# Transposes behind V products: the order of TensorE's work within a step of four attention mixers

## The chip, the cores and the metric

One core of one Trainium2 chip runs the whole program. The metric is device time in microseconds (us), lower is better; a time of a kernel is the median of several executions. A core has a matrix engine (TensorE, PE in the profile, its weight loads PEld), a vector engine (VectorE, DVE), a scalar engine (ScalarE, ACT), GpSimd (POOL) and SyncE (SP), each with its own instruction queue worked in program order, synchronized by semaphores.

## What is computed

Two transformer blocks over 512 tokens of width 1024. The change lies in the second block, in its softmax mixers: differential attention, attention with a forget gate ("fox"), and sparse attention ("nsa") with three branches (compressed, selected, window). All have this form, cut from the reference:

```python
# differential attention: two softmax maps per head
s = jnp.einsum('bhqmd,bhkmd->bhmqk', qb, k) * scale + bias;  p = softmax(where(dist >= 0, s, NEG))
w = p[:, :, 0] - lam * p[:, :, 1]
o = jnp.einsum('bhqk,bhkd->bhqd', w, v)
# forgetting attention: bias is cq - cum; one map per head
# sparse attention: o = g0 * softmax(cmp) @ vc + g1 * softmax(sel) @ v_slc + g2 * softmax(win) @ v_win
```

## The kernel before

The mixers' work is a list `MIX` of 40 items. An item is one block of 128 queries (`t` of 0 to 3), for one pair of heads (e = 0, 1), against w = (t+1)*128 keys. The order of the blocks is t = 3, 0, 2, 1, so the widths are 512, 128, 384, 256. Items 0 to 7 are differential ("diff", four score maps each: two per head), 8 to 15 fox (two maps), 16 to 39 nsa: for each of two pairs of heads and each t, a compressed branch of 31 keys ("cmp"), then the selected and the window branch of width w (two maps each).

Each engine runs a loop over steps n and works on items of different age:

- TensorE, `mixers_pe` (L1929): `scores(MIX[n])` writes each map to one of four PSUM banks (L1938); `turn(MIX[n-2])` transposes the probabilities in 128x128 pieces into banks 4 (e = 0) and 5 (e = 1) (L1950); `times_v(MIX[n-3])` multiplies V by the turned probabilities into bank 6 or 7 (L1961). At n = 0 it also spreads the forget gate (L1972).
- VectorE, `mixers_dve` (L1979): `front(n)` adds the bias to the scores and takes the row's minimum of the negated sum (L1992), writing into `SRING`, a ring of 8 maps; `back(n-1)` makes reciprocals and probabilities (L1999 to L2022).
- ScalarE, `mixers_act` (L2031): `exps(n)` (L2039), then `keep(n-2)`, the copies of the turned probabilities from banks 4 and 5 to `PTR`, which has two buffers (L2048), then `keep_out(n-4)`, the output of a pair of heads (L2054).
- GpSimd, `fox_bias_pool` (L2069): the biases of the fox items, two buffers (L2080, L2082); its third item waits until `front` of the first fox item has read its own.

The waits that tie them: `scores` waits until `front` has read the bank four maps before. `turn(n-2)` waits, for each half e, for the probabilities of item n-2 (`mx_probs`) and for `mx_kept` of item n-3's half e, since it writes the bank which that copy empties. `times_v(n-3)` waits for both copies of item n-3 (`mx_kept`, 2n+2 by its own n). `front` waits, from map 8 on, for the transposes (`mx_turned`) of the item that used its place in the ring eight maps before: for diff items, item n-2. `keep` waits for its transposes and for the V products two items before.

After the mixers follow a fourth mixer (stick-breaking, `stick_pe`) and the rest of the block.

Of the kernel before, what the change touches and what calls it, by code (L numbers as in the profile page):

```python
# [159 lines left out]
def build_program(nc, A, out):  # L160

    ctx = ExitStack()
    with ctx:
# [1464 lines left out]
        def cst2(name):  # L1628
            o, w = c2_at[name]
            return C2[:, o:o + w]  # L1630
# [292 lines left out]
        MIX = mixer_items()  # L1923
# [5 lines left out]
        def mixers_pe(pe):  # L1929

            sel4 = cst2("sel4").rearrange("p (h m) -> p h m", h=4)

            def scores(it):
                for k, (l, r, _) in enumerate(it["maps"]):
                    j = it["j0"] + k
                    if j >= 4:
                        pe.wait_ge(mx_shifted, j - 3)
                    nc.tensor.matmul(ps[:, j % 4, 0:it["w"]], l, r, start=True, stop=True).then_inc(mx_scores, 1)  # L1938

            def turn(it):  # L1940
                n = it["n"]
                for e in range(2):
                    pe.wait_ge(mx_probs, 2 * n + e + 1)
                    if n == 0:
                        pe.wait_ge(fox_kept, 4)
                    else:
                        pe.wait_ge(mx_kept, 2 * n + e - 1)
                    src = SRING[:, (it["j0"] + e) % 8, :]
                    for i, (c0, m) in enumerate(it["blocks"]):
                        last = nc.tensor.transpose(ps[0:m, 4 + e, i * P:(i + 1) * P], src[:, c0:c0 + m], ident)  # L1950
                    last.then_inc(mx_turned, 1)

            def times_v(it):
                n, t = it["n"], it["t"]
                pe.wait_ge(mx_kept, 2 * n + 2)
                if it["begins"] and it["pair"] >= 2:
                    pe.wait_ge(mx_out_kept, it["pair"] - 1)
                nb = len(it["blocks"])
                for x, (c0, m) in enumerate(it["blocks"]):
                    for e in range(2):  # L1960
                        last = nc.tensor.matmul(ps[64 * e:64 * e + 64, 6 + it["pair"] % 2, t * P:(t + 1) * P],  # L1961
                                                it["v_of"](e, x), PTR[0:m, n % 2, e, x, :],
                                                start=it["begins"] and x == 0, stop=it["ends"] and x == nb - 1)
                last.then_inc(mx_pv, 1)

            for n in range(len(MIX) + 3):
                if n < len(MIX):
                    scores(MIX[n])
                if n == 0:

                    for h in range(4):
                        nc.tensor.matmul(ps[:, 4 + h, :], sel4[0:4, h, :], FL[0:4, 1, :], start=True,  # L1972
                                         stop=True).then_inc(fox_spread, 1)
                if 2 <= n < len(MIX) + 2:
                    turn(MIX[n - 2])
                if n >= 3:
                    times_v(MIX[n - 3])

        def mixers_dve(v):  # L1979

# [495 lines left out]
        def _(eng):  # L2476
# [46 lines left out]
            qk_norm_pe(pe)  # L2523
            pe.stage_end()
            mixers_pe(pe)
            pe.stage_end()
            stick_pe(pe)
# [41 lines left out]
```

## Time and profile before

| | us |
|---|---|
| median of 3 runs | 1983.44 |
| lowest, highest of them | 1979.52, 1989.31 |
| the profiled execution's own time | 1981.9 |
| its span, first to last instruction | 1979.8 |
| the mixers' steps in it (L1938 to L1961) | 118.5 |
| TensorE busy in the span | 1746.8 |
| VectorE busy | 946.2 |
| ScalarE busy | 624.8 |

The profile is of one execution. A row of the timeline has start, duration, engine, line, operation, output and inputs, shapes, count, and in brackets the idle time of the engine before it with what ended it. TensorE's ends are modelled, so its busy time is not work at its peak; starts are what to read. Where several instructions were merged, the row gives the first start and the count.

### The profile page before, as it was taken

To read this page: it belongs to the slowest core of one execution; us is meant where nothing else is said; L and a number is where in the kernel's file an instruction comes from. 1 tells how busy PE (TensorE), PEld (TensorE's weight loads), DVE (VectorE), ACT (ScalarE), POOL (GpSimd) and SP (SyncE) were. 2 spreads that over 40 slices of the span, in tenths; PEclk is the share of its full clock that TensorE was granted. 3 is DMA by queue.
4 is the path that set the end of the run, shared out by engine and by line. 5 is a ranking of instruction groups with operands and counts; after the bars stand their busy time and mean duration, and the time that the engine had idled before them with its cause. 6 is when DMAs were issued, how large, how long until landed. Compare 5 with 4: busy or idle time off the path is not lost.

```text
span 1979.8 us, 26555 instructions
## 1 busy us (share of the span) xinstructions
PE 1746.8 (88%) x11544; PEld 1400.2 (71%) x11544; DVE 946.2 (48%) x1447; ACT 624.8 (32%) x900; POOL 34.4 (2%) x50
## 2 busy tenths in 40 slices
PE   3999765986889889999999689998876879999998
PEld 2888434983779578888888478875544768888886
DVE  4135658623334434555454632245754455554644
ACT  2221143224233415424231122244764222222220
POOL 0000000000000000000000000001300000000000
PEclk9999887997999999999999899976987889999999
DMA  4322200001224133455454422320000223323322
GB/s 136 102 89 88 85 12 1 4 4 34 73 64 154 39 127 109 143 176 183 135 201 160 134 64 75 97 44 1 1 1 0 66 63 86 107 86 106 88 93 74
DMA packets 149029, 163.62 MB, mean 83 GB/s; under 512 B 14704, under 2 KB 110306, under 8 KB 148786
## 3 DMA queue, kind: packets, MB, share of 16 engines
q1 hardware_dynamic: 141896, 152.10, 24.2%
q10 hardware_dynamic: 7018, 9.83, 1.7%
q8 instruction: 91, 1.49, 0.3%
q14 instruction: 24, 0.20, 0.0%
HBM read 159.79 MB, written 2.13 MB: 82 GB/s over the span
## 4 chain that ended last, share of the span: by engine, by line
PE 74%; DVE 6%; ACT 4%; issue 2%; POOL 1%; DMA 1%; DVEq 1%; ACTq 0%; POOLq 0%
PE ps L370 54%; PE ps L1031 4%; PE ps L1157 2%; PE ps L630 2%; PE ps L2121 1%; PE ps L1950 1%; PE ps L1938 1%; PE ps L1961 1%; PE ps L1335 1%; PE ps L1811 1%; POOL sb_hT L2080 1%; DVEq L156 1%; PE ps L1767 1%; ACT sb_hT L2039 1%; PE ps L1809 1%
## 5 line engine op out<-in xcount | busy, mean ns | idle before, releaser
L390 DVE TENSOR_TENSOR weights_low<-sb_weights_raw,weights_high 128x2048 fp32r<-128x2048 f32 (+3 forms) x119 | 266.6, 2241 | 376.5 <-ACT weights_high L387 376.2
L370 PE MATMUL ps<-left_high,weights_high 128*128 128x512 f32 x1032 | 405.4, 393 | 19.0 <-DVEq L156 7.5
L370 PE MATMUL ps<-left_low,weights_high 128*128 128x512 f32 x1032 | 403.9, 391 | 0.0
L370 PE MATMUL ps<-left_high,weights_low 128*128 128x512 f32 x1032 | 403.6, 391 | 0.0
L387 ACT CAST weights_high<-sb_weights_raw 128x2048 fp32r<-128x2048 f32 (+3 forms) x119 | 222.2, 1868 | 446.4 <-PE ps L370 437.6
L370 PEld LDWEIGHTS ps<-left_high,weights_high 128*128 128x128 f32 x1032 | 193.7, 188 | 61.9 <-DVEq L156 8.1
L370 PEld LDWEIGHTS ps<-left_high,weights_low 128*128 128x128 f32 x1032 | 193.7, 188 | 42.7
L370 PEld LDWEIGHTS ps<-left_low,weights_high 128*128 128x128 f32 x1032 | 193.9, 188 | 41.6
L370 PE MATMUL ps<-weights_high,hidden_high 128*128 128x512 f32 x432 | 168.9, 391 | 0.0
L370 PE MATMUL ps<-weights_high,hidden_low 128*128 128x512 f32 x432 | 168.2, 389 | 0.0
L370 PE MATMUL ps<-weights_low,hidden_high 128*128 128x512 f32 x432 | 168.1, 389 | 0.0
L370 PE MATMUL ps<-weights_high,left_high 128*128 128x512 f32 (+2 forms) x352 | 125.6, 357 | 26.1 <-DVE left_low L649 26.1
L370 PE MATMUL ps<-weights_low,left_high 128*128 128x512 f32 (+2 forms) x352 | 125.1, 355 | 0.0
L370 PE MATMUL ps<-weights_high,left_low 128*128 128x512 f32 (+2 forms) x352 | 124.9, 355 | 0.0
L370 PEld LDWEIGHTS ps<-weights_high,left_high 128*128 128x128 f32 x352 | 67.9, 193 | 37.3 <-issue 28.0
L370 PEld LDWEIGHTS ps<-weights_high,hidden_low 128*128 128x128 f32 x432 | 81.1, 188 | 17.1
L370 PEld LDWEIGHTS ps<-weights_high,hidden_high 128*128 128x128 f32 x432 | 81.1, 188 | 16.7
L370 PEld LDWEIGHTS ps<-weights_low,hidden_high 128*128 128x128 f32 x432 | 81.1, 188 | 16.5
L1534 DVE TENSOR_TENSOR hidden_low<-sb_arena,hidden_high 128x512 fp32r<-128x512 f32 x54 | 37.4, 692 | 92.4 <-ACT hidden_high L1529 92.4
L370 PEld LDWEIGHTS ps<-weights_low,left_high 128*128 128x128 f32 x352 | 67.9, 193 | 9.2
L370 PEld LDWEIGHTS ps<-weights_high,left_low 128*128 128x128 f32 x352 | 67.8, 193 | 9.3
L630 PE MATMUL ps<-sb_arena,sb_X 128*128 128x128 f32 x320 | 47.1, 321 | 30.0 <-DVE sb_arena L599 30.0
(342 smaller groups left out, 2167.3 us busy)
## 6 DMA issues: line engine op xcount, KB each, us to landing
sb_weights_raw<-in_w_in SPq DMA_DIRECT2D x24, 1024.0 KB, 5.3
sb_yT<-in_ada_w SPq DMA_DIRECT2D x24, 1024.0 KB, 5.2
sb_weights_raw<-in_ffn_w_up SPq DMA_DIRECT2D x44, 512.0 KB, 4.8
sb_weights_raw<-in_mlp_w_up SPq DMA_DIRECT2D x16, 1024.0 KB, 6.0
sb_weights_raw<-in_mlp_w_down SPq DMA_DIRECT2D x16, 1024.0 KB, 7.4
sb_weights_raw<-in_ffn_w_down SPq DMA_DIRECT2D x10, 1024.0 KB, 5.0
sb_weights_raw<-in_w_out SPq DMA_DIRECT2D x8, 1024.0 KB, 5.0
sb_weights_raw<-in_xattn_w_kv SPq DMA_DIRECT2D x8, 1024.0 KB, 5.3
```

The source lines that it names most:

```text
L156: self.eng.drain().then_inc(self.stage_sem, 1)
L370: last = nc.tensor.matmul(o, lhsT, rhs, start=b["first"] and i == 0, stop=b["last"] and i == len(pairs) - 1)
L387: nc.scalar.copy(h[:, 0:n], raw[:, 0:n]).then_inc(w_high, 1)
L390: nc.vector.tensor_tensor(l[:, 0:n], raw[:, 0:n], h[:, 0:n].bitcast(F32), ALU.subtract).then_inc(w_low, 1)
L630: last = nc.tensor.matmul(ps[:, k, t * P:(t + 1) * P], src[:, t, k * P:(k + 1) * P], RDIAG[:, t, :], start=True, stop=True)
L1031: last = nc.tensor.matmul(ps[b, bank, c * 64:(c + 1) * 64], lhsT(b, u, c), rhs(b, u, c), start=True, stop=True)
L1157: last = nc.tensor.matmul(o_of(b), *own_pairs[i], start=i == 0, stop=i == len(own_pairs) - 1)
L1335: last = nc.tensor.matmul(ps[b, 6 + o % 2, q0:S], v_of(x), PT[0:m, buf, x, q0:S], start=grp["begins"] and x == 0, stop=grp["ends"] and x = ...
L1534: nc.vector.tensor_tensor(HIDL[part % 2][:, i, :], x, HIDH[part % 2][:, i, :].bitcast(F32), ALU.subtract).then_inc(ff_low, 1)
L1767: last = nc.tensor.matmul(ps[:, 4 * (i % 2) + f, :], mat, SQS[i][:, f, :], start=True, stop=True)
L1809: nc.tensor.matmul(ps[b, 1, 0:1], PHI[b, l, :], PET[b, l:l + 1], start=l == 0, stop=l == 31)
L1811: last = nc.tensor.matmul(ps[b, 2, 0:NCMP], PHI[b, l, :], KV[b, l:l + 16 * (NCMP - 1) + 1:16], start=l == 0, stop=l == 31)
```

## The change

In each step TensorE's V products of item n-3 now stand ahead of the transposes of item n-2; they stood behind them. Nothing else is changed: the waits inside `turn` and `times_v` are the same, and so are the loops of the other engines.

```diff
@@ mixers_pe, for n in range(len(MIX) + 3): after scores(MIX[n]) and, at n == 0, the forget gate's spread
+                if n >= 3:
+                    times_v(MIX[n - 3])
                 if 2 <= n < len(MIX) + 2:
                     turn(MIX[n - 2])
-                if n >= 3:
-                    times_v(MIX[n - 3])
```

## Rows read from the trace of the kernel before

**Rows 1.** The page's first line: the span.
```profile
span 1979.8 us, 26555 instructions
```

**Rows 2.** View by windows, the mixers' steps: window, its length, busy us of each engine.
```profile
1345.57:1464.11 118.54, 101.36 (x728) 60.74 (x728) 81.21 (x336) 80.49 (x282) 26.05 (x32) 0.86 0.00 1
```

**Rows 3.** Waits in that window: who waited for whom, us, times, longest.
```profile
DVE sb_hT L1992 <- PE ps L1938: 22.3, 22, 4.6
...
PE ps L1950 <- ACT sb_hT L2048: 9.1, 15, 1.3
```

**Rows 4.** View by windows, two stretches; the granted clock is third from last.
```profile
1360.00:1365.00 5.00, 3.75 (x12) 2.29 (x10) 3.21 (x13) 3.45 (x10) 2.16 (x5) 0.50 0.00 0
...
1380.00:1385.00 5.00, 3.67 (x28) 2.22 (x26) 3.57 (x16) 3.45 (x10) 0.00 (x0) 1.00 0.00 0
```

**Rows 5.** Timeline, step 3: keep(0), T(1), V(0), front(3).
```profile
1363.55 1.04 ACT L2048 COPY sb_hT<-ps 128x512 f32<-128x512 f32 x2
...
1364.25 0.93 PE L1950 MATMUL ps<-sb_consts,sb_hT 128*128 128x128 f32 x2 [0.45 <-ACT sb_hT L2048]
...
1365.11 1.98 PE L1961 MATMUL ps<-sb_hT,sb_arena 128*64 128x128 f32 x16
1365.33 0.42 DVE L1992 CUSTOM_DVE_ANT_0 sb_hT<-ps,sb_arena 128x256 f32<-128x256 f32 x1 [1.54 <-PE ps L1950]
```

**Rows 6.** Timeline, step 4: T(2); step 5: keep(2), T(3), V(2)'s loads.
```profile
1369.04 0.64 PEld L1950 LDWEIGHTS ps<-sb_consts,sb_hT 128*128 128x128 f32 x6 [1.50 <-DVE sb_hT L2013]
...
1373.64 0.83 ACT L2048 COPY sb_hT<-ps 128x384 f32<-128x384 f32 x2
...
1374.23 1.08 PE L1950 MATMUL ps<-sb_consts,sb_hT 128*128 128x128 f32 x4 [0.79 <-ACT sb_hT L2048]
1375.25 1.15 PEld L1961 LDWEIGHTS ps<-sb_hT,sb_arena 128*64 128x64 f32 x12 [0.33 <-issue]
```

**Rows 7.** Timeline, step 6: keep(3), T(4).
```profile
1377.36 0.61 ACT L2048 COPY sb_hT<-ps 128x256 f32<-128x256 f32 x2
...
1378.32 1.51 PE L1950 MATMUL ps<-sb_consts,sb_hT 128*128 128x128 f32 x8
```

**Rows 8.** Timeline, step 7: keep(4), T(5)'s second half.
```profile
1383.00 1.04 ACT L2048 COPY sb_hT<-ps 128x512 f32<-128x512 f32 x2
...
1384.18 0.30 PE L1950 MATMUL ps<-sb_consts,sb_hT 128*128 128x128 f32 x1 [0.18 <-ACT sb_hT L2048]
```

**Rows 9.** Timeline, GpSimd: first and last of 24 in the fox items.
```profile
1390.30 1.40 POOL L2080 TENSOR_SCALAR sb_hT<-sb_yT,sb_small 128x384 f32<-128x384 f32 x1 [27.96 <-DVE sb_stat L1992]
...
1410.08 0.45 POOL L2082 TENSOR_TENSOR sb_hT<-sb_hT,sb_arena 128x128 f32<-128x128 f32 x1
```

**Rows 10.** Timeline, T(17); then steps 31 to 35: T(29), S, V(29), keep(28) to keep(30).
```profile
1419.37 1.06 PE L1950 MATMUL ps<-sb_consts,sb_hT 128*128 128x128 f32 x8 [0.87 <-DVE sb_hT L2020]
...
1443.32 0.40 ACT L2048 COPY sb_hT<-ps 31x128 f32<-31x128 f32 x2
...
1443.71 1.06 PE L1950 MATMUL ps<-sb_consts,sb_hT 128*128 128x128 f32 x8 [0.65 <-DVE sb_hT L2020]
...
1444.43 1.07 ACT L2048 COPY sb_hT<-ps 128x512 f32<-128x512 f32 x2
...
1446.51 0.85 PEld L1961 LDWEIGHTS ps<-sb_hT,sb_arena 128*64 128x64 f32 x16 [0.17 <-issue]
...
1446.71 1.05 ACT L2048 COPY sb_hT<-ps 128x512 f32<-128x512 f32 x2
1447.53 0.30 PEld L1938 LDWEIGHTS ps<-sb_arena 64*128 64x128 f32 x4 [0.17 <-issue]
...
1450.39 0.30 PEld L1938 LDWEIGHTS ps<-sb_arena 64*128 64x128 f32 x4 [0.17 <-issue]
```

**Rows 11.** Timeline, the drain: T(39), V(39)'s loads.
```profile
1462.20 0.69 PE L1950 MATMUL ps<-sb_consts,sb_hT 128*128 128x128 f32 x4
...
1463.40 0.42 PEld L1961 LDWEIGHTS ps<-sb_hT,sb_arena 128*64 128x64 f32 x8 [0.17 <-ACT sb_hT L2048]
```

## Prediction

> **What bounds the kernel now.** The page gives the span, 1979.8 us [rows 1]. The view by windows puts the changed loops in 118.5 us of it, 1345.57 to 1464.11 [rows 2]; nothing outside runs code that moves. So the question is what 118.5 us become. Below, S(n) are the score products of item n, T(n) its transposes, V(n) its V products; front(n) and back(n) are VectorE's halves, exps(n) and keep(n) ScalarE's. TensorE's step n was S(n), T(n-2), V(n-3) and becomes S(n), V(n-3), T(n-2).
>
> In that window TensorE's modelled busy time is 101 us, VectorE's 81, ScalarE's 80 [rows 2]: no engine is full, they hand work round. The list of waits says how. VectorE waits 22.3 us for scores, and 15 times, 9.1 us in all, the transposes' first matmul waits for keep (L2048) [rows 3]. This second row is the one to read: T(n-2) needs keep(n-3) because it writes the two PSUM banks that keep(n-3) empties (bank 4+e only after half e), and V(n-3) needs both halves of keep(n-3). Where T already starts the moment half 0 is kept, V cannot slip in ahead without pushing it.
>
> **The change, part by part.** Instructions are the same, 40 S, 40 T and 40 V groups, with the same durations, no DMA. No wait is added in name; but V's wait for both halves of keep(n-3) now stands ahead of T(n-2). Behind it on TensorE's queue are T(n-2) and S(n+1). SP's and POOL's queues are not passed. Three waits hang on T: keep(n-2); in the diff items (4 maps of a ring of 8) front(n), which needs T(n-2); and the last V of all.
>
> New closed loop: T(n) then keep(n), both halves, then V(n), then T(n+1). Old loop: T(n) half e, keep(n) half e, T(n+1) half e. So V and a half copy are added wherever this loop is what sets the time.
>
> *Diff items, steps 3 to 8.* The loop here is front, exps, keep, T, front.
> Step 3: keep(0) ends at 1363.55+1.04=1364.59, T(1) starts at 1364.25 behind its first half, V(0) follows, front(3) starts at 1365.33 [rows 5]. After: V(0) can start about 0.16 after keep ends (T(5)'s second half starts 0.14 after keep(4) does [rows 8]), at 1364.75, and its 16 matmuls hold TensorE some 1.85 of the 1.98 us shown at the low clock; T(1)'s second half, which started at about 1364.75 before, comes with 0.17 between the groups at about 1366.8. Front(3) moves by **+2.0**.
> Step 5: keep(2) ends at 1374.47, T(3) started at 1374.23, V(2)'s loads took 1.15 us [rows 6], and front(5) waits for T(3). After: V(2) from 1374.63 for 1.15 to 1.28, T(3)'s second half at about 1376.1 instead of 1374.7. **+1.3**.
> Step 6: T(4) starts at 1378.32, keep(3) ended at 1377.97 [rows 7]. V(3), 8 matmuls of about 0.053 us each at the full clock (16 take 0.85 [rows 10]), goes from 1378.13 to 1378.55; with 0.17 us between two groups [rows 10] T(4) comes at 1378.72. **+0.5**.
> Step 7: keep(4) ends at 1384.04, T(5)'s second half at 1384.18 [rows 8]; 16 V matmuls hold 0.85 [rows 10]. After: V(4) takes T(5)'s place, T(5) at 1385.2. **+1.1**.
> Steps 4 and 8: T(2) started at 1369.04 on VectorE's last probabilities, after 1.50 us without a load [rows 6], and T(6) likewise; keep plus the short V (0.20 us) ends before that, so V fits; I take +0.1 for both. Sum of the diff items **+5.0**. Bounds: if the clock is full in steps 3 and 5, V(0) costs half and the sum is 3.6; if low in all, V(3) and V(4) cost twice and the sum is 6.4.
>
> *Fox items.* POOL builds the bias tiles from 1390.30 to 1410.53 with no gap over 0.1 us [rows 9], and front waits for them at the end. POOL's start hangs on front(8), so the +5.0 passes on whole, but nothing is added: 0 (upper bound 0.8, if front(10) is late for the fifth pair of tiles). This is the cover; were it gone, T's in steps 9 to 15 would be late as in the next part.
>
> *Nsa items: two periods of 12 steps, 24.3 us each.* I walk the second, items 28 to 39; the first has the same rows 24.34 us earlier (T(17) at 1419.37, T(29) at 1443.71 [rows 10]). Step 31: keep(28) ends at 1443.72, T(29) starts at 1443.71 [rows 10]; V(28), four small matmuls, now goes ahead from 1443.88, and T(29) starts at 1444.35, +0.64. Keep(29), before at 1444.43 for 1.07 us, starts when T's first half is done, 1445.0, and ends 1446.1. Step 32: V(29) must wait for that, 1446.25, and hold 0.85; before, T(30) ran during keep(29). T(30) comes at 1447.27, S(33) at 1448.3 against 1447.53: +0.8. Step 33: keep(30) starts at 1447.87 against 1446.71, takes 1.05, V(30) ends at 1449.95, T(31) follows, S(34) at 1450.48: +1.2. Step 34: T(31), its keep of 0.4, V(31) and T(32) in a row; S(35) at 1451.75 against 1450.39: +1.4. From there VectorE's chain leads, and steps 37 and 38 add 0.2 in the same way. A period adds **+1.6**, two, less 0.1 counted twice at the seam, **+3.1**. Bounds: 0.8 a period if only step 32's exposed wait stays (later ones soaked by VectorE), 2.2 if the late S(35) also pushes the 384-wide pieces: 1.6 to 4.4 in all.
>
> *The drain.* T(39) at 1462.20, then keep(39), then V(39)'s second load block at 1463.40 [rows 11], 1.2 us after T. After: V(37) stands ahead of T(38) (+0.55) and V(38), which waits for keep(38), ahead of T(39), which comes at about 1463.7; V(39) at 1464.9. **+1.5** (bounds 0.6, V(37) and V(38) alone, and 1.8).
>
> **Sum.** 5.0 + 0 + 3.1 + 1.5 = 9.6 us, lost. The profiled execution took 1981.9 us, span 1979.8; 1981.9 + 9.6 = 1991.5. The three runs' median, 1983.44, is 1.5 above that execution, so about 1992 to 1993; I say **1992**. A 0.5% difference, 9.9 us, is about what a measurement of this kernel can tell from none (its own three runs lie 9.8 us apart).
>
> **The clock.** Granted clock is 0.50 (1.2 GHz) from 1360 to 1365, and 1.00 (2.4 GHz) from 1380 to 1385 [rows 4]; the climb lies within the stage, and every group of matmuls there costs twice at the low level (16 V matmuls: 1.98 against 0.85 [rows 5, 10]). The change adds idle TensorE time in just these steps; the sum keeps each step's clock as it was. The Trainium skill (TensorE: Matmul & The Clock Gate, "What's actually happening") says that the throttled state is the default and activity releases it. The rows agree: the low level follows the sparse steps before. By that rule extra idle time would postpone the climb, and the loss would be the 12 to 18 us of the third rival below in place of 9.6.
>
> **Rivals.**
> *V fills the idle time (not slower).* TensorE stood waiting for probabilities before most T. If V fits there, S(n+1) starts earlier by V's time and VectorE's waits for scores, 22.3 us in 22 times [rows 3], shrink. Some 16 of them are in the nsa items; by V's load time, 0.85 us for 512 keys [rows 10] and so 0.2 for 128, some 0.4 in the mean over all items, that is -6.4: 1975.5. It decides where keep(n-3) ends a full V before back(n-2). For: steps 4 and 8, and the wait by VectorE on scores. Against: the 15 T's that waited for keep itself [rows 3], and step 32, where T used the time of keep. Chance 0.05.
> *Absorbed.* VectorE's chain or POOL takes up the nsa part and half of the diff part: 0 to +5, about 1984.5. For: POOL's full 20 us; ScalarE's and VectorE's loads near 70%. Against: front(n) hangs on T(n-2) in the diff items with no slack. Chance 0.17.
> *The clock climbs later.* If the window up to about 1385 stays at 0.50, the bounds above give 6.4 for the diff items, the 26 transposes of T(2) to T(6) take up to 0.053 more each, 1.4, and S(4) to S(8) up to about 0.5 a step, an estimate: another 4, and 6.4 + 4 + 3.1 + 1.5 = 15: +12 to +18, about 1997. Chance 0.18.
> *My case*, +5 to +12: 0.60, with its own range 1987 to 1994.
>
> **How the numbers follow.** Over 9.9 us slower: 0.43 of my case (0.26), nearly all of the clock's (0.16): 0.42. Faster by over 0.5% needs more than the first rival gives: 0.02. The rest, 0.56, is within 0.5%. Range: 1983 (leaves out the first rival and a third of the second) to 2000 (leaves out the clock's upper end).
>
> **What would show it.** In the profile after: V(0) (L1961) ahead of T(1) (L1950), front(3) (L1992, 128x256) about 2 us later after keep(0); T waiting less for ScalarE, V now waiting for it (L1961 <- ACT L2048), which before it hardly did; POOL's 20.2 us unchanged; nsa period near 25.9 us instead of 24.3; the rest of the kernel as long as before. Wrong if the nsa period is no longer, if the window 1345 to 1380 has another clock, or if front in the diff items starts at the same distance from keep.

## The result and the profile after

The changed kernel takes 1995.84 us (median of 7 executions; one of them, of 2650 us at a mean clock of 0.64 and not 0.93, is left out of the comparison, and so is one of 3824 us of the filled new order below), the kernel before 1981.61 in the same comparison. The ratio is 1.0068, 95% interval 1.0047 to 1.0089: 14 us or 0.7% slower. That is inside the stated range, and beyond the 9.6 us of the likeliest case.

The profiled execution has a span of 1991.5 us. The view by windows for the mixers' steps, from the first score product to the start of the last output copy (columns as in [rows 2]; the granted clock is third from last):

```profile
1343.54:1477.28 133.74, 110.68 (x728) 67.43 (x728) 81.15 (x336) 81.80 (x281) 26.02 (x32) 0.77 0.00 1
```

133.74 us stand against 118.54 [rows 2]: +15.20, at a mean clock of 0.77 against 0.86. VectorE, ScalarE and GpSimd have the same busy time within 1.3 us. Outside the stage the two executions differ by -3.5 us (it begins 2.03 earlier, the rest behind it is 1.47 shorter), in code that is the same.

The list of waits in that window answers [rows 3]:

```profile
PEld ps L1961 <- ACT sb_hT L2048: 35.7, 39, 2.7
DVE sb_hT L1992 <- PE ps L1938: 28.3, 22, 4.6
PE ps L1961 <- ACT sb_hT L2048: 17.5, 24, 2.4
DVE sb_hT L1992 <- PE ps L1950: 16.2, 6, 3.6
...
ACT sb_hT L2048 <- PE ps L1950: 8.2, 14, 1.2
```

TensorE's wait for ScalarE's copies has moved from the transposes to the V products. The two rows with L1961 are two views of the same waits, those of the weight loads (PEld) and those of the matmuls behind them (PE), and can't be added: there are only 40 groups of V products. The loads of 39 groups wait, 35.7 us in all; the matmuls wait 17.5 us in 24 times, against 9.1 us in 15 times for the transposes before [rows 3]. (The "53 us in 63 times" of an expectation below is the sum of both rows.) Two more rows show who pays for it: VectorE's front waits 16.2 us for transposes (7.6 before), in 6 times, and ScalarE's copies 8.2 (0.9 before).

**The diff items.** Timeline, step 3, to be read against [rows 5]:

```profile
1361.52 1.04 ACT L2048 COPY sb_hT<-ps 128x512 f32<-128x512 f32 x2
...
1362.61 1.58 PEld L1961 LDWEIGHTS ps<-sb_hT,sb_arena 128*64 128x64 f32 x16 [1.55 <-ACT sb_hT L2048]
...
1364.52 0.69 PE L1950 MATMUL ps<-sb_consts,sb_hT 128*128 128x128 f32 x2
...
1365.36 0.42 DVE L1992 CUSTOM_DVE_ANT_0 sb_hT<-ps,sb_arena 128x256 f32<-128x256 f32 x1 [3.60 <-PE ps L1950]
```

V(0) starts when the second copy ends (1362.56), holds TensorE for 1.91 us to T(1)'s start, and front(3) comes 3.84 us after keep(0) began; before it was 1.78: +2.06. Here is the view by windows from each front to the next, steps 3 to 8, after:

```profile
1358.51:1365.36 6.85, 5.25 (x26) 3.80 (x26) 3.22 (x14) 3.45 (x10) 1.62 (x4) 0.50 0.01 2
1365.36:1371.38 6.02, 5.40 (x18) 3.12 (x18) 3.57 (x13) 2.43 (x10) 0.00 (x0) 0.50 0.00 1
1371.38:1378.58 7.20, 5.22 (x24) 3.85 (x24) 4.15 (x14) 3.66 (x10) 0.00 (x0) 0.50 0.00 0
1378.58:1384.30 5.72, 5.22 (x24) 3.42 (x24) 3.35 (x13) 2.17 (x10) 0.00 (x0) 0.51 0.00 0
1384.30:1391.15 6.85, 4.72 (x26) 3.04 (x26) 3.22 (x13) 3.45 (x10) 0.00 (x0) 0.74 0.00 0
1391.15:1396.36 5.21, 4.72 (x16) 2.49 (x18) 3.49 (x14) 2.86 (x11) 0.00 (x0) 0.50 0.00 0
```

and the same of before (these windows were not among the rows above):

```profile
1360.54:1365.33 4.79, 3.69 (x12) 2.51 (x14) 3.22 (x14) 3.45 (x10) 1.62 (x4) 0.50 0.00 0
1365.33:1370.07 4.74, 4.74 (x34) 2.72 (x32) 3.57 (x14) 2.43 (x10) 0.00 (x0) 0.61 0.02 5
1370.07:1375.47 5.40, 3.70 (x18) 2.23 (x16) 4.15 (x14) 3.67 (x10) 0.00 (x0) 0.72 0.00 0
1375.47:1379.99 4.52, 4.52 (x32) 2.94 (x32) 3.35 (x14) 2.17 (x10) 0.00 (x0) 0.58 0.00 0
1379.99:1384.63 4.64, 3.31 (x22) 1.86 (x20) 3.21 (x13) 3.45 (x10) 0.00 (x0) 1.00 0.00 0
1384.63:1388.89 4.26, 3.17 (x30) 1.77 (x26) 3.49 (x14) 2.87 (x11) 0.00 (x0) 1.00 0.00 0
```

The steps lose 2.06, 1.28, 1.80, 1.20, 2.21 and 0.95 us, 9.50 in all. VectorE's and ScalarE's busy times are equal row by row, within 0.01 us. The clock column is not: before, it reaches 1.00 in step 7; after, it stays at 0.50 or 0.51 to step 6 and is back at 0.50 in step 8.

The prediction took the 1.50 us without a load ahead of T(2) [rows 6] for a gap into which V(1) fits. The timeline of TensorE's matmuls before, in steps 4 and 8, shows that only one of the two steps has it:

```profile
1367.02 2.10 PE L1938 MATMUL ps<-sb_arena 32*128 32x512 f32 x8
1369.04 0.88 PE L1950 MATMUL ps<-sb_consts,sb_hT 128*128 128x128 f32 x6
...
1387.68 1.08 PE L1950 MATMUL ps<-sb_consts,sb_hT 128*128 128x128 f32 x6 [1.09 <-DVE sb_hT L2013]
```

In step 4 the loads had stopped, but S(4)'s matmuls ran until T(2) began: no idle time. After the change V(1) starts at 1369.07, as S(4) ends, and T(2) 0.62 us behind it. Ahead of T(6), in step 8, the matmuls stood idle for 1.09 us.

**The fox items.** GpSimd's first and last rows, against [rows 9]:

```profile
1397.77 1.40 POOL L2080 TENSOR_SCALAR sb_hT<-sb_yT,sb_small 128x384 f32<-128x384 f32 x1 [37.47 <-DVE sb_stat L1992]
...
1417.68 0.45 POOL L2082 TENSOR_TENSOR sb_hT<-sb_hT,sb_arena 128x128 f32<-128x128 f32 x1
```

20.36 us, before 20.23. GpSimd starts 54.2 us after the first score product (44.7 before) and adds 0.13: a full cover.

**The nsa items and the drain.** Steps 31 to 35, against [rows 10], and the drain, against [rows 11]:

```profile
1453.26 1.09 PE L1950 MATMUL ps<-sb_consts,sb_hT 128*128 128x128 f32 x8
...
1454.01 1.07 ACT L2048 COPY sb_hT<-ps 128x512 f32<-128x512 f32 x2 [0.43 <-PE ps L1950]
...
1454.29 0.30 PEld L1938 LDWEIGHTS ps<-sb_arena 64*128 64x128 f32 x4 [0.17 <-issue]
...
1455.14 0.85 PEld L1961 LDWEIGHTS ps<-sb_hT,sb_arena 128*64 128x64 f32 x16 [0.55 <-ACT sb_hT L2048]
...
1456.16 0.85 PEld L1950 LDWEIGHTS ps<-sb_consts,sb_hT 128*128 128x128 f32 x8 [0.17 <-DVE sb_hT L2020]
...
1457.18 0.30 PEld L1938 LDWEIGHTS ps<-sb_arena 64*128 64x128 f32 x4 [0.17 <-issue]
...
1460.64 0.30 PEld L1938 LDWEIGHTS ps<-sb_arena 64*128 64x128 f32 x4 [0.17 <-issue]
...
1465.90 1.02 PEld L1950 LDWEIGHTS ps<-sb_consts,sb_hT 128*128 128x128 f32 x6 [0.17 <-issue]
...
1475.35 0.42 PEld L1950 LDWEIGHTS ps<-sb_consts,sb_hT 128*128 128x128 f32 x4 [0.17 <-issue]
...
1475.88 0.65 ACT L2048 COPY sb_hT<-ps 128x256 f32<-128x256 f32 x2 [1.17 <-PE ps L1950]
...
1476.58 0.42 PEld L1961 LDWEIGHTS ps<-sb_hT,sb_arena 128*64 128x64 f32 x8 [0.81 <-ACT sb_hT L2048]
```

Behind S(32) V(29) waits 0.55 us for the end of keep(29), time in which T(30) ran before. From T(29) to S(35) it takes 7.38 us, before 6.68. From T(17) at 1427.50 to T(29) at 1453.26 one period takes 25.76 us, before 24.34: +1.42. Near the end T(35)'s six loads, at 1465.90, take 1.02 us and not the 0.64 of the full clock: it dips there. What the dip costs can be read from the same kernel, since T(23) to T(24), one period earlier, are the same instructions. View by windows, T(23) to T(24), then T(35) to T(36):

```profile
1440.14:1442.50 2.36, 2.32 (x25) 1.57 (x23) 1.45 (x8) 1.49 (x5) 0.00 (x0) 1.00 0.00 0
1465.90:1469.71 3.81, 3.81 (x24) 2.66 (x22) 1.79 (x9) 1.96 (x7) 0.00 (x0) 0.55 0.02 4
```

That is 1.45 us at a clock of 0.55. T(39) to V(39) is 1.23 us, before 1.20; what is added stands ahead of T(39). From GpSimd's last end to the stage's end it is 59.15 us against 53.58: +5.57. With 9.50 and 0.13 that makes the 15.20. Of the 5.57 us, 1.45 are the dip's, and 4.12 are left for the order.

### The profile page after: what moved, and what is told of

Its sections match the earlier page's. It is cut to its first block, busy times and chain, and to the rows that moved or that the text cites. A ratio compares the mean times of both kernels' runs of the same rounds, so it can differ in the third digit from the quotient of the medians.

```text
span 1991.5 us, 26555 instructions
## 1 busy us (share of the span) xinstructions
PE 1751.8 (88%) x11544; PEld 1404.7 (71%) x11544; DVE 946.1 (48%) x1447; ACT 626.0 (31%) x900; POOL 34.3 (2%) x50
## 4 chain that ended last, share of the span: by engine, by line
PE 74%; DVE 6%; ACT 4%; issue 2%; DMA 1%; POOL 1%; DVEq 1%; ACTq 0%; POOLq 0%
PE ps L370 54%; PE ps L1031 4%; PE ps L1157 2%; PE ps L630 2%; PE ps L1961 1%; PE ps L2121 1%; PE ps L1938 1%; PE ps L1950 1%; ACT sb_hT L2039 1%; PE ps L1335 1%; PE ps L1811 1%; DVEq L156 1%; PE ps L1767 1%; ACT sb_hT L2048 1%; PE ps L1809 1%
```

## The experiments

Two theories. *L*: the closed loop of copy, V products, transposes puts V's own time on the path wherever the loop leads. *C*: what costs is TensorE's clock. And, within L, whether it is the wait for the second copy or the time of V behind it.

**Where the loss lies.** The new order in some steps only:

```diff
+                if n >= 3 and (n <= 8):      # second kernel: (n >= 16)
+                    times_v(MIX[n - 3])
                 if 2 <= n < len(MIX) + 2:
                     turn(MIX[n - 2])
-                if n >= 3:
+                if n >= 3 and not (n <= 8):
                     times_v(MIX[n - 3])
```

> V products stand ahead of transposes in steps 3 to 8 only. If each part of the loss comes from its own steps (theory L, the closed loop of copy, V products, transposes), GpSimd starts on the fox biases some 9 us later after the first score product than before (44.7 us before, 54.2 after the change), the nsa period stays at 24.3 us, and the kernel is about 9.5 us slower than before. If the loss of the diff items is mostly a clock that would climb late by chance (theory C), it is between 3.6 and 5 us when the clock climbs as in the kernel before.

> V products stand ahead of transposes from step 16 on only. Theory L: GpSimd's start stays at 44.7 us after the first score product, the nsa period is 25.8 us instead of 24.3, the drain 1 to 1.5 us longer, 4 to 5.5 us slower in all. Theory C (only the clock's late climb costs): no measurable loss, since the clock is at its full level there.

> The changed kernel once more, for the granted clock. If its clock (0.50 until 1380 us, 0.50 again from 1390 to 1401) is a consequence of the order, it is the same within a few us here; if it is chance, the climb lies elsewhere and the diff items take 3 us or more less.

Steps 3 to 8 alone: ratio 1.0060 (1.0045 to 1.0075), some 12 us; GpSimd starts 54.2 us after the first score product, as in the changed kernel. Step 16 on alone: 1.0042 (1.0027 to 1.0057), some 8 us, GpSimd at 44.6. The whole change again: 1.0077 (1.0060 to 1.0094). The placing that theory L gives is right. But the parts add to more than the whole (1.010), and the nsa part was expected at 4 to 5.5 us. The view by windows from GpSimd's last end to the stage's end, before, then steps 3 to 8 alone, then step 16 on alone, shows why:

```profile
1410.53:1464.11 53.58, 47.92 (x434) 30.22 (x434) 38.31 (x184) 41.36 (x157) 0.01 (x1) 1.00 0.01 2
1419.33:1476.00 56.67, 50.86 (x434) 31.96 (x434) 38.28 (x184) 41.51 (x156) 0.00 (x1) 0.94 0.01 2
1410.90:1472.66 61.76, 52.76 (x434) 33.19 (x434) 38.25 (x184) 42.82 (x156) 0.00 (x0) 0.92 0.01 2
```

The changed kernel took 59.15 us there, at 0.97. With only steps 3 to 8 changed, the nsa items have the order of before and yet lose 3.09 us, at a clock of 0.94; with step 16 on changed they lose 8.18 where the whole change lost 5.57. In both a lower clock goes with the surplus, which neither theory had placed there.

The second profile of the changed kernel repeats its steps 3 to 8 to 0.01 us, the clock of each to 0.01, and so does that of steps 3 to 8 alone. The late climb is thus most likely a consequence of this instruction order: C in its form "by chance" falls; as a consequence of the order it remains.

**The wait without V's time, and V's time without the wait.** First the kernel before with one wait more:

```diff
                 n = it["n"]
+                if n:
+                    pe.wait_ge(mx_kept, 2 * n)
                 for e in range(2):
                     pe.wait_ge(mx_probs, 2 * n + e + 1)
```

> The kernel before with one more wait: the transposes of item n-2 wait for both copies of item n-3, not for the half that they overwrite. V products stay behind. This is the new order's wait without V's time ahead. If the wait is the cost, GpSimd's start moves by most of the 9.5 us; if V's time behind that wait is, by 0 to 2 us (a half copy of 0.2 to 0.5 us at steps 3, 5 and 7), and the nsa period by under 0.5 us.

Steps 3 to 8 took 28.53 us in sum, against 28.35 before and 37.85 after: the wait costs the diff items 0.2 us. In the second nsa period and the drain, all at the full clock, S(28) to the end of V(39) takes 28.2 us against 27.6. Over the kernel the ratio is 1.0023 (1.0013 to 1.0032), some 4.5 us, more than the 0 to 2 us and the half microsecond a period lead to. The first nsa period shows where most of that comes from. The view by windows, from S(19) to S(22), items 19 to 21, in this kernel, and the same of before:

```profile
1415.80:1425.84 10.04, 9.14 (x69) 7.00 (x67) 4.81 (x26) 6.50 (x24) 0.00 (x0) 0.66 0.00 0
```

```profile
1418.09:1424.98 6.89, 6.02 (x69) 4.65 (x67) 4.85 (x27) 6.23 (x24) 0.00 (x0) 1.00 0.00 0
```

The same 69 matmuls; their mean clock fell to 0.66 and the three items took 3.15 us longer. The wait as such is small where the clock is as before; a fall of the clock is not.

Then V one item older, whose copies were made a step before:

```diff
-            for n in range(len(MIX) + 3):
+            for n in range(len(MIX) + 4):
...
+                if n >= 4:
+                    times_v(MIX[n - 4])
                 if 2 <= n < len(MIX) + 2:
                     turn(MIX[n - 2])
-                if n >= 3:
-                    times_v(MIX[n - 3])
```

> V products of item n-4 instead of n-3 stand ahead of the transposes of item n-2, so that their wait for both copies is over long before. Theory L: the loss is gone, TensorE's wait of V for the copies (53 us in 63 times after the change) falls to nearly nothing, and V fills idle time: from 0 to 6 us faster than the kernel before. The rival, that V ahead of T costs by its place alone (TensorE's time ahead of the transposes), has it still 3 us or more slower than before.

Ratio 1.0011 (0.9999 to 1.0022): within noise of before, and 11 us faster than the changed kernel. The wait of V's loads for copies is down from 35.7 us to 9.5. But it isn't the gain of 0 to 6 us that was expected: in the diff items step 4, where V(0) now stands ahead of T(2), takes 7.32 us instead of 4.74 at a clock of 0.50 (0.61 before), steps 3 to 8 take 33.81 instead of 28.35, and GpSimd starts at 50.2 us. V(0) follows S(4) there without a pause and holds TensorE for 1.91 us: V's time costs with no wait before it, so the rival named in the expectation holds in these steps. In the nsa items it gains 1.9 us from GpSimd's last end on (51.72 against 53.58): from S(28) to the end of V(39) 26.4 against 27.6, while S(16) to S(28) takes 25.1 against 24.7, with a clock of 0.67 in one stretch of 5 us.

**V's time twice.** The changed kernel with the V products of items 0 to 5 issued two times over:

```diff
+                for _ in range(2 if n < 6 else 1):
-                for x, (c0, m) in enumerate(it["blocks"]):
+                    for x, (c0, m) in enumerate(it["blocks"]):
...
```

> The changed kernel with the V products of items 0 to 5 (steps 3 to 8) issued twice. If V's time stands on the path in each of these steps, the six steps grow by V's slots once more: 1.9, 0.6, 1.3, 0.9, 1.7 and 0.3 us at the low clock, near 6.5 in sum, or 3.5 if the denser work raises the clock. If the loss was the wait ahead of V and not its time, they grow by under 1.5 us in all.

The ratio to before is 1.0091 (1.0061 to 1.0120), in two executions. Steps 3 to 8 took 8.55, 5.51, 8.34, 6.20, 8.00 and 4.50 us, 41.10 in sum, 3.25 more than after, near the 3.5 expected if the clock rises. Step 3, at the same clock but for 0.01, grew by 1.70, about the time of one V(0) at 1.2 GHz. Steps 4 and 8 became shorter, at clocks of 0.79 and 1.00 in place of 0.50: with more work in TensorE's idle time the clock was back sooner. So V's time is on the path, and the clock hides part of it in the sum.

**The order at a high clock.** Matmuls whose output nobody reads were added to both orders, ahead of the mixers and in steps 1 to 6 or 7 (between S(n) and what follows it); first few, then more:

```diff
             last.then_inc(cmp_sum, 1)
+            for _ in range(4):
+                nc.tensor.matmul(ps[:, 6, :], ident, KV, start=True, stop=True)
             pe.wait_ge(cmp_sq, pe.count(cmp_sq))
...
+            FILL = {1: 2, 2: 1, 3: 1, 4: 1, 5: 1, 6: 1}   # more: {1: 3, 2: 1, 3: 2, 4: 2, 5: 3, 6: 2, 7: 2}
...
+                if n == 1:
+                    pe.wait_ge(fox_kept, 4)
+                for _ in range(FILL.get(n, 0)):
+                    nc.tensor.matmul(ps[:, 7, :], ident, QK[:, 0, :], start=True, stop=True)
```

> The kernel before with added matmuls whose output nobody reads (four of 512 columns ahead of the mixers, then two, one, one, one, one, one in the idle time of steps 1 to 6), to raise TensorE's clock in the diff items. This is the base of the pair for the order at a high clock. If fillers raise the clock, 1345 to 1385 us is at 1.00 and the stage is 0 to 4 us shorter; if not, it is up to 4 us longer.

> The changed kernel with the same fillers. If the order's own cost in the diff items is the 3.6 us that the prediction gave for the full clock and the other 6 are the clock's, GpSimd's start on the fox biases is 3 to 4.5 us later than in the filled old order; if the 9.5 us are the order's cost at any clock, it is 8 or more later.

> Old order with denser fillers (three, one, two, two, three, two, two in steps 1 to 7), to hold the clock at 1.00 through the diff items, where the first fillers let it fall in steps 5, 6 and 8. Base of a pair; front(5) to front(8) spaced as in the kernel before at the full clock (4.52, 4.64, 4.26 us), or up to 1 us more a step where a filler is in the way.

> New order with the same fillers. At clock 1.00 the first pair gave +1.08 us for step 3 and +0.52 for step 4 against +2.06 and +1.28 at 0.50. If the rest is the same, front(3) to front(8) loses 4 to 5 us in sum to the more filled old order where both clocks are at 1.00; if the order alone costs the 9.5 us, 8 or more.

As a means to a faster kernel the fillers fail: ratios 1.0056 (1.0041 to 1.0071) and 1.0061 (1.0038 to 1.0084) in the old order, 1.0137 (1.0119 to 1.0154) and 1.0135 (1.0115 to 1.0155) in the new. Nor did they hold the clock everywhere. But they give steps in which both orders run at 1.00. The windows of steps 3, 4 and 6 to 8, more filled, old order:

```profile
1366.12:1371.15 5.03, 4.41 (x18) 2.35 (x20) 3.21 (x13) 3.45 (x10) 0.00 (x0) 1.00 0.00 0
1371.15:1376.71 5.56, 5.56 (x38) 3.33 (x34) 3.57 (x14) 2.43 (x10) 0.00 (x0) 1.00 0.02 4
...
1384.83:1389.66 4.83, 4.83 (x36) 2.94 (x34) 3.34 (x13) 2.17 (x10) 0.00 (x0) 1.00 0.00 0
1389.66:1394.69 5.03, 4.85 (x26) 2.54 (x24) 3.21 (x13) 3.45 (x10) 0.00 (x0) 1.00 0.00 0
1394.69:1398.95 4.26, 3.17 (x30) 1.77 (x26) 3.49 (x14) 2.87 (x11) 0.00 (x0) 1.00 0.01 4
```

and new order:

```profile
1368.61:1374.82 6.21, 5.43 (x30) 2.90 (x30) 3.21 (x14) 3.45 (x10) 0.00 (x0) 1.00 0.01 3
1374.82:1380.89 6.07, 5.44 (x22) 2.68 (x22) 3.56 (x14) 2.43 (x10) 0.00 (x0) 1.00 0.01 1
...
1391.22:1396.79 5.57, 5.07 (x28) 2.88 (x28) 3.35 (x13) 2.17 (x10) 0.00 (x0) 1.00 0.00 0
1396.79:1404.64 7.85, 7.08 (x30) 3.33 (x30) 3.22 (x14) 3.45 (x10) 0.00 (x0) 0.78 0.01 2
1404.64:1408.92 4.28, 2.85 (x16) 1.63 (x18) 3.48 (x14) 2.86 (x11) 0.00 (x0) 1.00 0.00 0
```

At the full clock on both sides the order costs 1.18 us in step 3, 0.51 in step 4, 0.74 in step 6 and 0.02 in step 8; the first, less filled pair gave 1.08 and 0.52 for steps 3 and 4. Unfilled these four lost 2.06, 1.28, 1.20 and 0.95. So some 2.4 of 5.5 us are the order's own and the rest the clock's. This carries over to the unfilled kernels only as an estimate, since the fillers take time of their own and hide part of the waits. In steps 5 and 7 the two sides had different clocks, and their split wasn't measured. For the whole of steps 3 to 8 the expectations were missed: the new order is 7.9 us behind the old with the first fillers (37.77 against 29.84; expected were 3 to 4.5, or 8 and more) and 7.5 with more (40.31 against 32.83; expected 4 to 5, or 8 and more). In neither pair did both sides hold 1.00 throughout, so the sums decide nothing.

**A version that beats both.** The old order up to step 15, V one item older ahead of the transposes from step 16 on, where the clock is high:

```diff
+                if n > 16:
+                    times_v(MIX[n - 4])
                 if 2 <= n < len(MIX) + 2:
                     turn(MIX[n - 2])
-                if n >= 3:
+                if 3 <= n < 16:
                     times_v(MIX[n - 3])
```

> Old order up to step 15, and from step 16 on the V products of item n-4 ahead of the transposes of n-2. The nsa period with V one item older was 1.2 us shorter than before in the look at V one item older throughout, and the diff items were what lost. So 2 to 3 us faster than before if that holds, 0.15% at most; no change if the clock in the nsa items falls.

> The same with the fillers of the pair above in the diff items. Gains add: the filled old order's change to before plus 2 to 3 us less.

Ratio to before 0.9982 (0.9972 to 0.9991), 4.2 us faster by the medians (1976.78 against 1980.97), a little more than the 2 to 3 us expected; the interval lies below 1. From S(16) to S(28) it takes 22.6 us against 24.7. From GpSimd's last end to the stage's end it is 50.24 us against 53.58, both at a clock of 1.00. With fillers the ratio is 1.0032 (1.0021 to 1.0044), 4.2 us less than the filled old order: the gain adds as expected, but the fillers lose more than it gives back.

## Why the prediction was right in sign and short in size

- *No wait in name, but the wait for both copies ahead of the transposes; old and new loop.* Right. 39 of the 40 V groups wait for copies, and the two kernels with half of the change each place the loss as the steps do. The wait alone costs 0.2 us in the diff items; V's time behind it is what counts.
- *Step 3, +2.0.* 2.06. It is the one diff step whose clock was 0.50 on both sides.
- *Steps 4 and 8, +0.1 together.* 1.28 and 0.95. "V fits" holds for step 8 at the full clock (0.02) and not for step 4 (0.51 to 0.52), whose 1.50 us without a load were a pause of the loads and not of TensorE; the rest is the clock. The same two views are mixed in "costs twice at the low level (1.98 against 0.85)": 16 V matmuls take 1.98 and 1.09 us, their loads 1.58 and 0.85.
- *Steps 5, 6, 7: +1.3, +0.5, +1.1.* 1.80, 1.20, 2.21. At the full clock step 6 costs 0.74.
- *The diff items, +5.0, bounds 3.6 to 6.4.* 9.50. **This is the term that failed**, and the step of it is "the sum keeps each step's clock as it was". The prediction had seen that the change adds idle time of TensorE on the clock's way up, and gave that its own rival, with 6.4 + 4 us for these items; measured are 9.5. One of its own signs of being wrong came: from 1345 to 1380 us the clock is 0.50, where it was 0.56. The bounds of the term itself doubled V's cost alone and not that of the transposes behind it: T(2)'s loads take 1.14 us where they took 0.64.
- *The fox items, 0.* 0.13 us. GpSimd's chain passes the delay on and adds nothing.
- *A nsa period, +1.6.* +1.42 from T(17) to T(29), V(29)'s exposed wait in its place. From T(29) to S(35) the walk is right to 0.02 us (7.40, measured 7.38); the 0.2 too much lies behind it.
- *The drain, +1.5.* With both periods and the seam, 5.57 us against 4.6. The clock's dip around 1466 us accounts for 1.45 of them, by the same instructions a period earlier; without it, it would be 4.12. The sum has no term for a fall of the clock in the nsa items. All six profiles in which the new order reaches these items have a dip at T(35).
- *The sum, 9.6.* 15.20 in the stage of the profiled execution, 14.2 by the medians. The likeliest case (+5 to +12) was left on the upper side; the outcome is that of the third rival, +12 to +18, which had 0.18, and the time lies in the stated range because the range took that rival in. Once the first low-clock step loses 2 us, the later ones can't be costed at the clock of before.
- *V fills the idle time.* It does, if V is one item older and the clock is high: 22.6 against 24.7 us from S(16) to S(28). In the change as made V's copies are too young. *Absorbed*: only GpSimd's part.

The Trainium skill (TensorE: Matmul & The Clock Gate, "What's actually happening") has the throttled state as the default that activity releases; the prediction set 12 to 18 us beside that rule. In the diff items the trace agrees: 0.50 until step 6, where the denser kernel before had 1.00 from step 7 and the one with V twice 0.79 already in step 4. Ahead of them it doesn't, if busy time is that activity: before, the clock was 0.50 from 1320 to 1340 us with TensorE counted busy throughout (last section), so the prediction's "the low level follows the sparse steps before" isn't borne out.

Open: how steps 5 and 7 divide between order and clock; and why the clock fell in the nsa items of some kernels (such as those with the wait alone, with steps 3 to 8 changed, and changed from step 16) and not in others. In the two profiles of the changed kernel the dip is at the same instructions.

## What to carry to other kernels

Ahead of a stalled instruction, put only work whose own inputs were ready long before; work that waits for the same producer turns idle time into a longer loop. So ask of work put into a pause not only how long it is but how old its operands are: here one item more in age turned a loss of 14 us into no loss, and into a gain of 4 us where TensorE ran at its full clock. Look for the pause in the matmuls' rows and not in the loads'. And where a loop runs while the clock is on its way up, cost each step at the low level once the first one has slipped.

## What the runs showed of the hardware

- TensorE can be counted busy throughout and run at 1.2 GHz. View by windows: the kernel before, in the stage ahead of the mixers (194 matmuls of 64x31 and 64x1); then the old order with fillers, first the 512-column fillers with 128 rows, below it the score products and the forget gate's spread (tiles of 32 and of 4 rows).

```profile
1320.00:1340.00 20.00, 20.00 (x194) 20.00 (x193) 8.23 (x13) 4.69 (x5) 0.00 (x0) 0.50 0.01 2
...
1343.00:1348.00 5.00, 4.26 (x8) 1.47 (x7) 0.00 (x0) 0.69 (x2) 0.00 (x0) 0.72 0.00 0
1353.50:1359.50 6.00, 6.00 (x14) 2.50 (x13) 2.49 (x8) 4.46 (x11) 0.00 (x0) 0.50 0.00 1
```

  The profile counts TensorE busy for all of 20.00 and of 6.00 us at a granted clock of 0.50. Between the last two stretches lies a sparse one (1.29 us busy of 3.20 from 1348.0), behind which the clock is 0.50; the small tiles didn't bring it back. What about these matmuls leaves it low wasn't tried.
- The clock isn't quite set by the instruction stream. The version that beats both has the code of before up to step 15; in its profile GpSimd starts at 46.2 us and not at 44.7, with 0.79 and 0.54 for the clock of steps 7 and 8 where before has 1.00 and 1.00. The changed kernel repeated its own to 0.01. Differences of 1.5 us between single profiles of this kernel can come with the clock alone.
